# RWKV sequence: reads and writes of the sample states dealt between the output products of the head pairs

## The reference, cut to what matters

```
def step(s, inp):
    r_t, k_t, v_t, w_t, kk_t, a_t = inp
    s = (s * w_t[:, :, None, :]
         - jnp.einsum('bhij,bhj->bhi', s, kk_t)[..., None] * (kk_t * a_t)[:, :, None, :]
         + v_t[..., None] * k_t[:, :, None, :])
    return s, jnp.einsum('bhij,bhj->bhi', s, r_t)
```

## Time and profile before

| what | value |
| --- | --- |
| median of 3 runs | 2824.67 us (2823.83 to 2824.96) |
| the profiled execution, its own time | 2825.71 us |
| its span, first to last instruction | 2824.1 us |
| TensorE matmuls busy | 2502.8 us (89%) |
| VectorE, ScalarE, GpSimd busy | 1257.9, 913.9, 185.8 us |
| mean granted clock of TensorE | 0.926 |

### The profile page before, as it was taken

One profiled execution on the slowest core, in us unless ns is written; L12 is line 12 of the kernel. 1 busy time (PEld: TensorE's weight loads), 2 busy tenths in 40 slices (PEclk: granted clock), 3 DMA queues, 4 the chain that ended last, 5 costly groups with the idle time before them and its releaser, 6 DMA issues. The chain is left out here.

```text
span 2824.1 us, 57983 instructions
## 1 busy us (share of the span) xinstructions
PE 2502.8 (89%) x24330; PEld 2239.7 (79%) x24330; DVE 1257.9 (45%) x1932; ACT 913.9 (32%) x1404; POOL 185.8 (7%) x276
## 2 busy tenths in 40 slices
PE   3978989898999689999959789898989996899998
PEld 3868879675999477999958689796759985769998
DVE  4554443343666543333344644423436665433333
ACT  1432012444333443322124320124443334432221
POOL 0012110110011000000000121101101110000000
PEclk9989779999999899999979897799999998999999
DMA  4200613248223159565232006122482230686561
GB/s 142 75 17 4 218 47 101 77 124 295 71 81 91 34 129 261 187 220 200 83 120 62 18 4 221 56 91 74 146 273 79 84 95 19 156 234 224 190 229 63
DMA packets 267506, 345.53 MB, mean 122 GB/s; under 512 B 32116, under 2 KB 225878, under 8 KB 265656
## 3 DMA queue, kind: packets, MB, share of 16 engines
q1 hardware_dynamic: 245384, 328.13, 36.8%
q10 hardware_dynamic: 21856, 13.63, 1.8%
HBM read 322.65 MB, written 102.68 MB: 151 GB/s over the span
## 5 line engine op out<-in xcount | busy, mean ns | idle before, releaser
L411 PE MATMUL ps<-x_hi,w_hi 128*128 128x272 f32 x2304 | 685.8, 298 | 47.3 <-DVE w_lo L391 40.6
L411 PE MATMUL ps<-x_hi,w_lo 128*128 128x272 f32 x2304 | 676.7, 294 | 0.0
L411 PE MATMUL ps<-x_lo,w_hi 128*128 128x272 f32 x2304 | 675.5, 293 | 0.0
L411 PEld LDWEIGHTS ps<-x_hi,w_hi 128*128 128x128 f32 x2304 | 446.4, 194 | 59.0 <-issue 36.6
L391 DVE TENSOR_TENSOR w_lo<-ring,w_hi 128x1024 fp32r<-128x1024 f32 (+4 forms) x194 | 254.5, 1327 | 466.4 <-ACT w_hi L381 445.2
L411 PEld LDWEIGHTS ps<-x_lo,w_hi 128*128 128x128 f32 x2304 | 446.5, 194 | 0.9
L411 PEld LDWEIGHTS ps<-x_hi,w_lo 128*128 128x128 f32 x2304 | 445.6, 193 | 0.0
L381 ACT CAST w_hi<-ring 128x1024 fp32r<-128x1024 f32 (+4 forms) x194 | 214.1, 1126 | 174.1 <-PE ps L447 62.6
L460 PE MATMUL ps<-w_hi,x_hi 128*128 128x256 f32 (+1 forms) x480 | 137.0, 286 | 13.7 <-DVE x_lo L2777 13.7
L460 PE MATMUL ps<-w_hi,x_lo 128*128 128x256 f32 (+1 forms) x480 | 137.4, 286 | 0.0
L460 PE MATMUL ps<-w_lo,x_hi 128*128 128x256 f32 (+1 forms) x480 | 136.4, 284 | 0.0
(11 more groups left out here) (383 smaller groups left out, 4583.4 us busy)
## 6 DMA issues: line engine op xcount, KB each, us to landing
ring<-in_w_in_dram SPq DMA_DIRECT2D x44, 1024.0 KB, 5.4
ring<-in_w_in_dram SPq DMA_DIRECT2D x62, 512.0 KB, 4.2
c_rows<-in_cache_c_kv_dram SPq DMA_DIRECT2D x40, 768.0 KB, 13.7
out_c_kv_sample_dram<-in_cache_c_kv_dram SPq DMA_DIRECT2D x16, 1524.0 KB, 17.0
pages_early<-in_cache_b_k_dram SPq DMA_DIRECT2D x80, 256.0 KB, 3.8
pages_early<-in_cache_b_v_dram SPq DMA_DIRECT2D x80, 256.0 KB, 5.7
c_rows<-in_cache_c_kv_dram SPq DMA_DIRECT2D x32, 384.0 KB, 10.1
pages_more<-in_cache_b_k_dram SPq DMA_DIRECT2D x32, 256.0 KB, 3.8
```

Of the source, the lines that this page charges most:

```text
L411: last = pe.matmul(o[:, half, 0:HALF], self.w[w][:, i % 2, k, c * P:(c + 1) * P], self.x[x][:, k, half * HALF:(half + 1) * HALF], start=(k ...
```

## The change

`sample_writes` and the loop of the output products become one function, `outputs_and_samples`. Its four waits stand at its head. It goes through four blocks; block c issues the four output products of head pair c, and behind them, for samples 2c and 2c + 1, the read and the two writes. y_mm is raised by the last output product of block 3, x_mm by the last write, and the four own-token products with dy_mm come last. The matmuls are the same ones.

```
-            def sample_writes(p):
+            def outputs_and_samples(tile):
+
+                p = tile
                 pp = slice(p * P, (p + 1) * P)
+                pe.wait_ge(at_done, 4 * (tile + 1))
                 pe.wait_ge(du_done, p + 1)
-                for b in range(8):
-                    t = slice(SEQ + 4 * b, SEQ + 4 * b + 4)
-                    pe.matmul(dec_y[:, 4 * b:4 * b + 4], SS[:, b, :], rho[:, p, t], start=(b == 0), stop=False, skip_group_check=True)
+                pe.wait_ge(um_done, p + 1)
+                pe.wait_ge(vm_done, p + 1)
+                for c in range(4):
+                    o = [ps[64 * hh:64 * hh + 64, Y_BANK, c * P:(c + 1) * P] for hh in range(2)]
+                    for hh in range(2):
+                        h = 2 * c + hh
+                        pe.matmul(o[hh], U[:, tile % 2, h * HD:(h + 1) * HD], at[0][:, h, :], start=False, stop=False, skip_group_check=True)
+                        y_last = pe.matmul(o[hh], vT[:, tile, h * HD:(h + 1) * HD], at[1][:, h, :], start=False, stop=True, skip_group_check=True)
+                    if c == 3:
+                        y_last.then_inc(y_mm, 1)
+                    for b in (2 * c, 2 * c + 1):
+                        t = slice(SEQ + 4 * b, SEQ + 4 * b + 4)
+                        pe.matmul(dec_y[:, 4 * b:4 * b + 4], SS[:, b, :], rho[:, p, t], start=(b == 0), stop=False, skip_group_check=True)
+                        x = half_bank(b // 4)[:, b % 4, :]
+                        pe.matmul(x, beT[0:NDEC, 4, pp], Um[:, b, :], start=True, stop=False)
+                        x_last = pe.matmul(x, kaT[0:NDEC, 4, pp], Vm[:, b, :], start=False, stop=True)
+                x_last.then_inc(x_mm, 1)
                 for hh in range(2):
...
                 last.then_inc(dy_mm, 1)
-                pe.wait_ge(um_done, p + 1)
-                pe.wait_ge(vm_done, p + 1)
-                for b in range(8):
-                    o = half_bank(b // 4)[:, b % 4, :]
-                    pe.matmul(o, beT[0:NDEC, 4, pp], Um[:, b, :], start=True, stop=False)
-                    last = pe.matmul(o, kaT[0:NDEC, 4, pp], Vm[:, b, :], start=False, stop=True)
-                last.then_inc(x_mm, 1)
...
-                    pe.wait_ge(at_done, 4 * (tile + 1))
-                    for h in range(8):
-                        R, p = slice(64 * (h % 2), 64 * (h % 2) + 64), h // 2
-                        f = slice(h * HD, (h + 1) * HD)
-                        o = ps[R, Y_BANK, p * P:(p + 1) * P]
-                        pe.matmul(o, U[:, tile % 2, f], at[0][:, h, :], start=False, stop=False, skip_group_check=True)
-                        last = pe.matmul(o, vT[:, tile, f], at[1][:, h, :], start=False, stop=True, skip_group_check=True)
-                    last.then_inc(y_mm, 1)
-                    sample_writes(tile)
+                    outputs_and_samples(tile)
```

## The result

The changed kernel took 2874.48 us (2867.47 to 2878.19, 4 runs) where the kernel before took 2824.25 (4 runs, with one more than in the table ahead of the prediction): ratio 1.0175, 95% interval 1.0157 to 1.0192, so about 50 us slower. The side was forecast; the size was not, with 2850 as the likeliest time and 2868 as the end of the range. The profiled execution took 2877.16 us with a span of 2875.6, 51.5 longer than before's.

A forecast was written before the change was run, and what follows sets the result against it. TensorE, its clock alternating between 2.4 and 1.2 GHz, was taken to bound the stage. Per tile 10.8 + 2.8 - 10.45 = +3.15 us, eight tiles +25 on 2825.71, so 2850; own range 2828 to 2867, whole range 2795 to 2868.

The forecast's parts named there:

- The bound: In the RWKV sequence of both layers TensorE sets the pace, busy 116.7 of 124.6 us, its granted clock averaging 0.73.
- The shape changes: In the dealt piece, 17 more changes of matmul shape add 2.9 us per tile, making 10.8 us at full clock.
- The base: The piece of tile 0 as profiled before the change, 10.45 us, set against the dealt piece for all eight tiles.
- The waits: Outputs also wait for own-token u, its masked copy and masked v; semaphores of outputs and writes move: cost nothing.
- The clock: In the dealt piece the clock still falls to 1.2 GHz, leaving 3.3 us at the low level, 2.8 us more per tile.
- The sign for right: Clock 0.50 in or ending most dealt pieces; 12 to 16 us from first output to next tile's L1236; read-write gaps about 0.2.
- the place of the fall: Inside the dealt piece the clock falls 7.5 us after its start, where the eight tiles before had 5.1 to 6.4.
- factor 1.86: Slowdown at the low clock, from L1236's group: 1.90 us there against 1.02 at full clock.
- The clock holds: Rival, chance 0.25: recurring outputs keep the full clock through the piece and next tile's products: 2799 us, or 2785.
- the drains: TensorE drains at each of the piece's 20 shape changes, making it as thin as the work ahead of the falls.
- It cancels: Rival, chance 0.13: the clock falls in some tiles and holds in others, or falls with the last block: 2825 us.

The follow-up runs named there:

- the first experiment: The order of the kernel before, with only the changed kernel's four waits put at the head: 2825.79 us, ratio 1.0004 to the kernel before.
- the grouped kernel: Against the changed kernel, each of the four blocks does both reads, then all four writes: 2862.51 us, ratio 1.0139 to the kernel before.
- the stacked grouped kernel: Four blocks of outputs, both reads, both writes, each pair of 32-row writes made one 64-row matmul: 2799.38 us, ratio 0.9923 to the kernel before.
- two bursts and stacked writes: Against the kernel before, write pairs made 64-row matmuls; order half the outputs, writes, other outputs, reads, own-token products: 2772.73 us, ratio 0.9821.
- the old order: The order of the kernel before, with each pair of writes made one matmul over 64 rows: 2791.06 us, ratio 0.9889 to the kernel before.
- the reordering into two bursts: Against the kernel before, half the outputs, all unstacked writes, other outputs, reads, own-token products; VectorE waits for own-token products: 2809.85 us, ratio 0.9957.
- the 64-row kernel: Four blocks of outputs, both reads, then 64-row writes each issued twice, so 32 write records: 2845.31 us, ratio 1.0062 to the kernel before.

## Why the prediction was right and wrong

*The bound* was right: TensorE sets the pace, and its clock the stage's time.

*The shape changes* were right in kind and a little too dear: 10.8 us was worked out for the piece at the full clock, the first block gives 10.3. The burst of outputs in it takes 0.59 us (309.15 to 309.74), where the prediction has some 0.4; a quarter of its 1.95 us is 0.49.

The drain that the Trainium skill gives as a rule ("TensorEngine Tiling (Array Packing)", Key Properties) agrees with the rows at this fine dealing too: a read behind a change takes 0.32 us where one in a group takes 0.235.

*The base* was one tile's: the 10.45 us against which the prediction sets the dealt piece is tile 0's, and it takes it eight times. The eight pieces before take 79.6 us, 9.95 in the mean, so the same forecast over all tiles would have been +29 in place of +25.

*The waits* were right: free, by the first experiment.

*The clock* was right in direction: it falls inside the piece, in all eight tiles, what follows runs as before, and the loss lies in the piece. The sign for right, 12 to 16 us a piece, was met and mostly passed, with 15.6 to 17.0. **The step that failed is the place of the fall.** The prediction took 7.5 us after the start, "somewhat later than now, since outputs recur", and even the bad end of its range kept the 5.1 us of the earliest fall before. Measured are 1.6 to 3.5, 2.5 in the mean. The prediction's own term with that number gives 10.3 - 2.5 = 7.8 us left, 6.7 more at its factor 1.86, so 17.0 us a piece and +56 in all; 16.3 and +50.5 were measured, a factor of 1.77 in place of 1.86. The reason behind the step, "since outputs recur", did not hold. Dealing brings the thin work forward: the reads begin 0.6 us into the piece in place of 1.95, the writes 0.9 in place of 4.2. The runs with half the dealing tell the two apart. With the reads at the head and no outputs before them the clock was lost 1.7 to 3.0 us after the first read, so the outputs ahead of them had helped to hold it. With the reads dealt between the outputs and the writes kept out it fell at 4.8 to 6.7 us in seven of eight pieces, hardly sooner than before. With the writes dealt in as well it fell at 1.5 to 3.5 us, but for one of the sixteen pieces of the changed and the grouped kernel. So it is the writes among the outputs that moved the fall. How much of that is their 32 rows, their number or their changes of shape is settled in part only: with half the records and the same 12 changes as in the grouped run, six of eight pieces held, and with as many records of 64 rows four of eight held beyond 6 us.

*The rivals.* "The clock holds" had a chance of 0.25 and did not happen in this kernel. Another run shows that its mechanism exists: in the stacked grouped kernel the clock holds over one whole period in each layer, and the period is 22.3 us. Its piece is 2.9 us shorter than the estimate of 10.3; with that added it would be 25.2, an estimate near the "some 25 us" of the prediction. Against the rival the prediction named the drains, which make the piece thin. The piece was too thin, but the changes of shape alone do not make it so, since with 12 of them the stacked kernel holds and the grouped one does not. "It cancels" did not happen: no tile held.

The Trainium skill's rule that the low level comes with idle time ("TensorE: Matmul & The Clock Gate", Part 1) does not agree with the trace of the changed kernel, nor with that of the one before: TensorE was busy in 2.66 of the 2.66 us ahead of tile 0's fall, and in all eight pieces of each kernel it was busy from the first output product to the fall.

## What to carry to other kernels

Before dealing thin work (short streams, few rows, changes of shape) between dense work, ask what the mixture is like, not what the gaps are: dealt finely, it lost the clock here sooner than thin work in a group behind a dense run. Make thin work shorter first (here two matmuls of 32 rows made one of 64), and part what is left by whole runs of dense work, not by single matmuls: two bursts and stacked writes took 51 us off the kernel where four dealt blocks had added 50, and with the writes stacked, too, the old order was 8 us faster than dealt blocks and two bursts 18 us faster than the old order. Read the granted clock of each stretch with the time from its start to the fall, since the same instructions took 11.4 or 15.5 us by that alone.

## What the runs showed that was not expected

The order of a few matmuls within one piece moved the fall of the clock from 1.6 us after its start to 9.6 us, on an engine that was busy all the way to it (in the last tile of a layer, with two bursts, it fell at 9.7 and 10.0, and there TensorE had waited about 1 us behind the piece); the reordering into two bursts, with not a matmul fewer, was 13 us faster than the kernel before. And the dealing that lost 37 us in grouped blocks gained 24 on the kernel before once its writes were half as many. Why the 64-row kernel falls early in some tiles and late in others is open: the runs show both, not what chooses between them. The same split shows in single pieces of other runs: one late fall, at 6.5 us, in the grouped blocks, one early one, at 2.4, with the reads dealt.
